# Last MoE layer of a diffusion backbone: expert results added to their tokens by one-hot products on TensorE in place of scatter and gather

## What is computed

```python
def moe(h, w_router, b_router, w_e_gate, w_e_up, w_e_down):
    ...
    gates = jnp.einsum('nk,nke->ne', w_top,
                       jax.nn.one_hot(top_idx, N_EXPERTS, dtype=jnp.float32)).astype(h.dtype)
    y = jnp.zeros_like(h)
    for e in range(N_EXPERTS):
        he = jax.nn.silu(h @ w_e_gate[e]) * (h @ w_e_up[e])
        y = y + gates[:, e:e + 1] * (he @ w_e_down[e])
    return y
```

## Time and profile before

| | |
|---|---|
| three runs, us | 1532.34, 1530.07, 1532.04 (median 1532.04) |
| profiled execution, us | 1531.17 |
| its span, us | 1529.3 |
| busy share of the span | PE 91%, DVE 52%, ACT 44%, POOL 11% |
| chain that ended last | PE 83%, DMA 7%, DVE 5%, ACT 3% |
| read from HBM, written | 341.38 MB, 25.69 MB |

### The profile page before, as it was taken

One profiled execution on the slowest core, in us unless ns is written; L12 is line 12 of the kernel. 1 busy time (PEld: TensorE's weight loads), 2 busy tenths in 40 slices (PEclk: granted clock), 3 DMA queues, 4 the chain that ended last, 5 costly groups with the idle time before them and its releaser, 6 DMA issues.

```text
span 1529.3 us, 21505 instructions
## 1 busy us (share of the span) xinstructions
PE 1395.5 (91%) x8088; PEld 1049.5 (69%) x8088; DVE 800.0 (52%) x1312; ACT 670.1 (44%) x1104; POOL 166.9 (11%) x188
## 2 busy tenths in 40 slices
PE   5699999999998995899999992999998897999995
PEld 2378777886556873778888872998885695655641
DVE  1512335424774626799999974567427665111113
ACT  3532223224665315578888864563246633000001
POOL 4210110001330000041111102000000000000001
PEclk9699999999998997799999996999999898999998
DMA  8674565334882232699999984355332158999996
GB/s 294 230 276 150 193 206 192 91 94 154 261 258 82 84 124 90 202 383 390 397 377 376 368 320 172 107 147 174 107 114 69 56 166 335 415 415 415 415 415 248
DMA packets 116054, 357.96 MB, mean 234 GB/s; under 512 B 13889, under 2 KB 14210, under 8 KB 115330
## 3 DMA queue, kind: packets, MB, share of 16 engines
q1 hardware_dynamic: 91410, 272.86, 48.6%
q0 software_dynamic: 23984, 81.85, 15.1%
q10 hardware_dynamic: 576, 2.10, 0.3%
HBM read 341.38 MB, written 25.69 MB: 240 GB/s over the span
## 4 chain that ended last, share of the span: by engine, by line
PE 83%; DMA 7%; DVE 5%; ACT 3%; issue 2%; POOL 0%; SPq 0%; POOLq 0%; DVEq 0%; ACTq 0%
PE ps L578 19%; PE ps L580 18%; PE ps L579 18%; PE ps L1194 6%; PE ps L1216 3%; PE ps L844 3%; PE ps L977 2%; PE ps L1000 2%; PE ps L1177 2%; DMA w_raw<-in_w_ada 1%; DMA ring<-in_w_e_down 1%; DMA ring<-in_w_e_up 1%; PE ps L988 1%; PE ps L1134 1%; DMA ring_h<-in_w_e_down 1%
## 5 line engine op out<-in xcount | busy, mean ns | idle before, releaser
L574 DVE TENSOR_TENSOR w_lo<-w_raw,w_hi 128x1024 fp32r<-128x1024 f32 x224 | 270.1, 1223 | 309.5 <-ACT w_hi L570 307.9
L570 ACT ACTIVATE w_hi<-w_raw 128x1024 fp32r<-128x1024 f32 x224 | 235.5, 1058 | 321.4 <-PE ps L580 317.6
L578 PE MATMUL ps<-h_hi,w_hi 128*128 128x512 f32 (+1 forms) x704 | 249.3, 354 | 11.1 <-issue 5.7
L580 PE MATMUL ps<-h_hi,w_lo 128*128 128x512 f32 (+1 forms) x704 | 247.3, 351 | 0.0
L579 PE MATMUL ps<-h_lo,w_hi 128*128 128x512 f32 (+1 forms) x704 | 247.1, 351 | 0.0
L578 PEld LDWEIGHTS ps<-h_hi,w_hi 128*128 128x128 f32 x704 | 134.2, 191 | 33.7 <-issue 9.6
L580 PEld LDWEIGHTS ps<-h_hi,w_lo 128*128 128x128 f32 x704 | 134.1, 190 | 18.7
L579 PEld LDWEIGHTS ps<-h_lo,w_hi 128*128 128x128 f32 x704 | 134.3, 191 | 18.2
L574 DVE TENSOR_TENSOR w_lo_more<-w_raw,w_hi_more 128x1024 fp32r<-128x1024 f32 x96 | 114.9, 1222 | 4.5
L570 ACT ACTIVATE w_hi_more<-w_raw 128x1024 fp32r<-128x1024 f32 x96 | 101.2, 1060 | 21.7 <-PE ps L580 19.3
L549 POOL DMA_DIRECT2D w_raw<-in_w_ada x96 | 68.8, 724 | 356.7 <-PE ps L844 350.1
(11 more groups left out here) (303 smaller groups left out, 2510.7 us busy)
## 6 DMA issues: line engine op xcount, KB each, us to landing
w_raw<-in_w_ada POOLq DMA_DIRECT2D x96, 512.0 KB, 5.5
w_raw<-in_w_e_gate SPq DMA_DIRECT2D x64, 512.0 KB
w_raw<-in_w_e_up SPq DMA_DIRECT2D x64, 512.0 KB
w_raw<-in_w_e_down SPq DMA_DIRECT2D x64, 512.0 KB
w_raw<-in_w_in SPq DMA_DIRECT2D x56, 512.0 KB
ring<-in_w_e_up SPq DMA_DIRECT2D x40, 512.0 KB, 13.7
ring<-in_w_e_gate SPq DMA_DIRECT2D x38, 512.0 KB
w_raw<-in_w_gate SPq DMA_DIRECT2D x32, 512.0 KB
```

The costliest lines, as they stand in the source:

```text
L570: act.activation(whi(n), raw[:, slot(n), :, :], ACT.Copy).then_inc(hi_ready, 1)
L574: dve.tensor_tensor(wlo(n), raw[:, slot(n), :, :], whi(n).bitcast(F32), ALU.subtract).then_inc(lo_ready, 1)
L578: pe.matmul(acc, sh, mh, start=first, stop=False, skip_group_check=True)
L580: return pe.matmul(acc, sl, mh, start=False, stop=last, skip_group_check=True)
```

## The change

All sixteen experts go back to their tokens by the product. `HELD`, `store`, `gathered`, `weighed`, the scatters, the gathers, the zeroing of `yhalf` and the row numbers in `places` go. `weigh(p)` multiplies the picks of experts 2p and 2p+1 with their gates in place, once they were used; `turn_put(p)` turns them with 8 matmuls against the identity into `put_back` (two pairs deep), and `put(e)` adds expert e's four products to banks 4 to 7, which it now holds for the whole stage. So the rest has to do with banks 0 to 3: the transposed hidden goes into the second half of bank 1, down into bank 2 alone, and all fills that a copy empties (pick half a, pick half b, row steps, turn_put) go one after the other through bank 3, in the order of a list `fills`; each waits for the copy of the one before. The picks are done in two halves.

```diff
-HELD = NE - 2
-ROWSTEPS = 10
+ROWSTEPS = 9
+FIRST_RAW = 6
...
     def r_slot(n):
         k = n % RING
-        if k < 16:
-            return ring16[:, k, :, :]
-        if k < 20:
-            return ring_h[:, k - 12, :, :]
-        if k < 26:
-            return ring_g[:, k - 20 if k < 22 else k - 18, :, :]
-        return ring_h[:, k - 26, :, :]
+        if k < 6:
+            return ring_g[:, k if k < 2 else k + 2, :, :]
+        if k < 22:
+            return ring16[:, k - FIRST_RAW, :, :]
+        return ring_h[:, k - 18 if k < 26 else k - 26, :, :]
...
-        return ps[:, 5:7, :] if t == 0 else ps[:, 3:8:4, :]
+        return ps[:, 4 + 2 * t:6 + 2 * t, :]
+
+    fills = [("a", 0), ("b", 0), ("row", 0)]
+    for e_ in range(1, NE - 1):
+        if e_ % 2:
+            fills += [("put", e_ // 2), ("a", e_ // 2 + 1), ("b", e_ // 2 + 1)]
+        elif e_ <= 8:
+            fills += [("row", e_ - 1), ("row", e_)]
+    fills.append(("put", NE // 2 - 1))
...
                 for n, (kind, e, ch) in enumerate(r_stream):
-                    if n < RAW:
-                        sp.wait_ge(lo_ready, nb - RAW + n + 1)
-                    elif n == RAW:
+                    if n == 0:
+                        sp.wait_ge(m_l[i], KT)
+                    elif FIRST_RAW <= n < FIRST_RAW + RAW:
+                        sp.wait_ge(lo_ready, nb - RAW + n - FIRST_RAW + 1)
+                    elif n == FIRST_RAW + RAW:
                         sp.wait_ge(w_used, nb)
...
-        for r in range(2 * len(tiles[1])):
-            pool.dma_start(yrows[1][r * P:(r + 1) * P, :], zrow[:, :]).then_inc(pad_out, 16)
...
                 over = pool.value_load(most[0:1, 0:1], min_val=0, max_val=T)
                 for j in range(2):
-                    pool.wait_ge(e_out[i][j], 16 * (NE // 2))
-            else:
...
+                    pool.wait_ge(e_out[j], 16 * (NE // 2))
+            pool.wait_ge(rt_loc[i], 1)
             if i:
-                over = pool.value_load(most[0:1, 0:1], min_val=0, max_val=T)
+                pool.wait_ge(z_put, 2)
+            over = pool.value_load(most[0:1, 0:1], min_val=0, max_val=T)
...
+            def turn_put(p):
+
+                take_fill(pe, ("put", p))
+                pe.wait_ge(u_weighed, p + 1)
+                for t in range(2):
+                    for j in range(2):
+                        for q in range(2):
+                            m = pe.matmul(ps[HC * q:HC * (q + 1), 3, (2 * t + j) * P:(2 * t + j + 1) * P],
+                                          pick1[:, 2 + t, 2 * p + j, :], ident, start=True, stop=True, skip_group_check=True)
+                m.then_inc(u_t, 1)
...
             def put(e):
 
                 pe.wait_ge(u_y, NE + e + 1)
-                pe.wait_ge(l_c, ROWSTEPS)
+                pe.wait_ge(*copied(("put", e // 2)))
                 for t in range(2):
                     for q in range(2):
-                        m = pe.matmul(last_bank(t)[:, q, :], put_back[HC * q:HC * (q + 1), t, e - HELD, :],
-                                      ytile1[HC * q:HC * (q + 1), e % 2, :], start=e == HELD, stop=e == NE - 1,
+                        m = pe.matmul(last_bank(t)[:, q, :], put_back[HC * q:HC * (q + 1), (e // 2) % 2, t, e % 2, :],
+                                      ytile1[HC * q:HC * (q + 1), e % 2, :], start=e == 0, stop=e == NE - 1,
                                       skip_group_check=True)
...
+            def weigh(p):
+
+                chosen = pick1[:, 2:4, 2 * p:2 * p + 2, :]
+                dve.tensor_tensor(chosen, chosen, spread(gate_of[:, :, 2 * p:2 * p + 2].unsqueeze(3), [P, 2, 2, HC]),
+                                  ALU.mult).then_inc(u_weighed, 1)
```

More of the change, by code:

```diff
@@ L304, in build @@
     starts = small("starts", [P, NE], I32)
+    gate_of = small("gate_of", [P, 2, NE])
     tokr = small("tokr", [P, 4, 2], F32R)
@@ L354, in build @@
     h_out, y_free = sem("h_out"), sem("y_free")
-    e_out = [[sem(f"e_out_{i}_{j}") for j in range(2)] for i in range(DEPTH)]
+    e_out = [sem(f"e_out_{j}") for j in range(2)]
     picked = sem("picked")
     e_in = [sem("e_in_a"), sem("e_in_b")]
-    r_in = raw_in + [sem(f"r_in{k}") for k in range(RAW, RING)]
-    r_used, l_t, l_c = sem("r_used"), sem("l_t"), sem("l_c")
+    r_new = [sem(f"r_in{k}") for k in range(RING - RAW)]
+    r_in = r_new[:FIRST_RAW] + raw_in + r_new[FIRST_RAW:]
+    r_used, u_weighed = sem("r_used"), sem("u_weighed")
     e_xt, e_xh, e_xl, e_sig, e_he, e_ht, e_hh, e_hl, e_ya, e_yd = (
@@ L757, in _ @@
                 for j in range(2):
-                    pool.wait_ge(e_out[i][j], 16 * (NE // 2))
-            else:
[L761 to L777, removed]
+                    pool.wait_ge(e_out[j], 16 * (NE // 2))
+            pool.wait_ge(rt_loc[i], 1)
             if i:
-                over = pool.value_load(most[0:1, 0:1], min_val=0, max_val=T)
+                pool.wait_ge(z_put, 2)
+            over = pool.value_load(most[0:1, 0:1], min_val=0, max_val=T)
             with pool.If(over > CAP[i]):
                 if i == 0:
-                    pool.wait_ge(pad_out, 16 * (ROWS // P))
+                    pool.wait_ge(pad_out, 16 * (ROWS // P - T // P))
                     for t in tiles[i]:
@@ L1167, in down, with pick_tokens @@
                     m.then_inc(w_used, 1)
-            def turn_pair(p):
+            def pick_tokens(side, p):
+                take_fill(pe, (side, p))
                 pe.wait_ge(picked, 4 + p // 2 + 1)
[L1171 to L1175, removed]
+                for k in range(4):
+                    kt = k if side == "a" else 4 + k
+                    d0 = (kt // CK) * CK * P + kt % CK
                     for t in tl:
-                        m = pe.matmul(ps[:, 5 + k // 4, (k % 4) * P:(k % 4 + 1) * P], h2rows[:, t - 2, d0:d0 + CK * P - 1:CK],
+                        m = pe.matmul(ps[:, 3, k * P:(k + 1) * P], h2rows[:, t - 2, d0:d0 + CK * P - 1:CK],
                                       pick1[:, t, 2 * p:2 * p + 2, :], start=t == tl[0], stop=t == tl[-1],
@@ L1221, in last_rows @@
             def last_rows(k):
[L1222 to L1223 removed]
+                take_fill(pe, ("row", k))
                 if k == 0:
@@ L1226, in last_rows @@
                         h0 = HC * (f // 4)
-                        m = pe.matmul(ps[h0:h0 + HC, 7, (f % 4) * P:(f % 4 + 1) * P], spread(mod[1][:, 40 + f, 0:1], [P, HC]), ident,
+                        m = pe.matmul(ps[h0:h0 + HC, 3, (f % 4) * P:(f % 4 + 1) * P], spread(mod[1][:, 40 + f, 0:1], [P, HC]), ident,
                                       start=True, stop=True, skip_group_check=True)
[L1229 to L1234, removed]
                 else:
@@ L1599, in tokens_a, with row_copy, put_copy @@
             def tokens_a(p):
-                act.wait_ge(u_t, NE + p + 1)
+                wait_filled(act, ("a", p))
                 if p >= 2:
                     act.wait_ge(r_used, r_done("u", 2 * p - 3))
-                act.activation(xT1[:, p % 2, 0:4, :].rearrange("p k t -> p (k t)"), ps[:, 5, :], ACT.Copy).then_inc(u_xa, 1)
+                act.activation(xT1[:, p % 2, 0:4, :].rearrange("p k t -> p (k t)"), ps[:, 3, :], ACT.Copy).then_inc(u_xa, 1)
+            def row_copy(k):
+                if k == 0:
+                    dst = ga_half[:, :]
+                else:
+                    dst = token_major[:, (k - 1) // 2, ((k - 1) % 2) * CW:((k - 1) % 2 + 1) * CW]
+                    act.wait_ge(rt_loc[i], 1)
+                wait_filled(act, ("row", k))
+                act.activation(dst, ps[:, 3, :], ACT.Copy).then_inc(u_xa, 1)
+            def put_copy(p):
+                wait_filled(act, ("put", p))
+                act.activation(put_back[:, p % 2, :, :, :].rearrange("p t j n -> p (t j n)"), ps[:, 3, :], ACT.Copy).then_inc(u_xa, 1)
             def gated1(e):
@@ L1988, in places @@
                 link(ins)
-                link(dve.tensor_tensor(v(ta), v(ta), v(tb), ALU.add))
-                for t in range(2):
-                    dve.tensor_tensor(weighed[:, t, :, :, :], spread(pick1[:, 2 + t, HELD:, :].unsqueeze(2), [P, 2, 2, HC]),
-                                      spread(ta[:, 2 + t, HELD:].unsqueeze(2).unsqueeze(3), [P, 2, 2, HC]), ALU.mult)
+                link(dve.tensor_tensor(gate_of[:, :, :], v(ta), v(tb), ALU.add))
             dve.tensor_copy(loc[:, :, t0:], loc_f[:, :, t0:])
```

139 lines of the change are left out of this document (60 added, 79 removed).

## The result

The changed kernel takes 1555.68 us in the median (1552.76 to 1558.89, four runs), beside 1531.05 us (1529.42 to 1532.34, four runs) for the kernel before. The ratio on record is 1.0175, 95% interval 1.015 to 1.0199; the quotient of the two medians is 1.0161, in the same interval. The forecast was 1559.0, range 1551 to 1570. The profiled execution took 1556.32 with a span of 1554.5, 25.2 above the span of before; the forecast made it 27.0.

What follows compares the result with a forecast made beforehand. PE was taken to bound the stage, with 12.6 us of weight waits: 26.9 + 9.2 + 1.0 + 3.2 + 0.7 - 12.6 - 1.4 = +27.0, from 1532.04 us to 1559.0, range 1551 to 1570.

Steps and rivals of the forecast that it cites:

- The bound: Last expert stage: PE decides until 1453 us, then waits for weights; a lighter DMA load gives back at most 12.6 us.
- How the 12.6 would come back: Weight transfers: dropping scatters and gathers saves 9.2 us, six earlier chunks 7.5; of 16.7 together PE keeps 12.6.
- Puts: Expert stage on PE: 14 more puts at 1.92 us, nothing hidden, +26.9; bounds 25.1 and 29.0 (one more 0.15 entry each).
- Turning the picks: Expert stage on PE: eight turn_puts at 1.22 us, less 0.59 for the old weighed step, +9.2; bounds -2.6 and +6.1.
- Halves of the picks: Picks in two halves: 0.15 us per separate entry, seven times, +1.0; bounds 0 and 2.1, if leaving costs as much.
- the one that said a put's 1.92 has both of its ends in it: Whether leaving a tiling mode is paid makes no difference for a put, whose 1.92 us runs from gate to up.
- The start: Stage start: half b waits 0.75 us for a copy, turn_put(0) 1.7, pick 1 0.7; +3.2 in all.
- rival 1: Clock: the 0.75 us break keeps PE at 1.2 GHz through gate 0 and up 0, giving 1566 us; chance 8%.
- POOL at the end of layer 0: Load of `most` moves behind the last store's wait, ahead of the gathers layer 1 waits for: +0.7 us (0 to 0.9).
- Tail: Kernel end: the first sum can start when half of the last put is done, -1.4 us (0 to 1.4).
- 2 (a put costs more in mid-stream): Each mid-stream put and turn_put costs two entries of 0.15 to 0.3 more, 24 steps: +7, 1566 us; chance 7%.
- 3 (overlap with the neighbours): Puts and turns overlap neighbouring tiles and the saved waits win, not slower; 1523 us if they cost nothing; chance 4%.

Runs made afterwards that it cites:

- third variant: Kernel before with 14 weight chunks allowed before w_out's products end, not 8, and without its 14 scatters and 4 gathers: 1516.96 us, ratio 0.9922.
- two puts variant: Changed kernel with puts for experts 14 and 15 alone, turn_puts and their copies kept: 1533.88 us, ratio 1.0035 to the kernel before.
- variant with the old ring: Changed kernel with 8 weight chunks issued before w_out's end, as in the kernel before: 1557.66 us, ratio 1.0191 to the kernel before.
- the order alone: Changed kernel with hidden transposes back behind the next gate, and places and weigh(0) ahead of hidden_copy(0): 1552.57 us, ratio 1.0167 to the kernel before.

## Why the prediction was right, point by point

- **The bound.** Right: PE's own work is 214.2 us from gate 0 to the last put (third variant), and whatever the DMA engines save is capped by the 12.4 above it (-12.6 was predicted, all of it as waits; some 1.4 of it is the low clock behind them). The changed kernel's stage is 38.8 above this floor; the sum had 39.5.
- **How the 12.6 would come back.** Half wrong, without harm to the sum. The prediction credited the two edits with 9.2 and 7.5 us. Alone they gave 11.6 and 2.35. It had not asked whether the ring had room for the early chunks: it is full before gate 0.
- **Puts.** +26.9 predicted; 1.92 each in place, 26.7 with the pair at the end (3.63 for two).
- **Turning the picks.** +9.2 predicted, 1.11 + 7 x 0.87 - 0.59 = 6.6 measured. The term was sized from L1227, and 0.87 is at the lower bound that was taken from up (0.9). L1227's 1.22 has one record of gate 1 (0.11) in it, so it was read a little too high. Its eight matmuls fill one column half after the other, turn_put alternates between the halves; that this makes the rest of the difference is likely, but no variant changed the order alone. This is the largest error of size.
- **Halves of the picks.** +1.0 predicted; 4.16 for 3.97 seven times is 1.3.
- **Missing: the ends of the new groups.** Two steps failed: the one that said a put's 1.92 has both of its ends in it, and the one that priced the halves by their entries alone and let leaving them be free. Before, each expert had one group in the dear form (up 3.60, behind the transposes) and one in the cheap form (gate 3.45, behind a down). Now both are dear: the gate follows the transposes, the up a put or half a pick. At even experts the two puts variant shows it from the other side: a put's absence gives 2.06, not 1.92. And moving the transposes back, which makes the gate 3.45 again, wins nothing in the early pairs. 14 gates at 0.15 make 2.1, and what is left of the stage's +26.4 after 26.7 + 6.6 + 1.3 + 2.15 - 12.4 is 2.0. (The 0.15 that four row steps now pay more and four transposes less do cancel, as the prediction had it.) The sum's own upper bound for the puts, one more 0.15 each, came true in its size.
- **The start.** +3.2 predicted: 0.75, 1.7 and 0.7. Measured 2.08, 1.46 and 0.69, 4.2 in all. The excess is rival 1 in part: half b stayed at 1.2 GHz (granted clock 0.50, 3.78 us for 2.15), though gate 0 ran at the high clock (1.00). The variant with the old ring, same code here, ran half b in 2.15 and needed 7.42 from pick 0 to gate 0. So this cost comes and goes with the run.
- **POOL at the end of layer 0.** +0.7 predicted, and misread: the change leaves the old load of `most` where it was and adds a second one behind the wait. The timeline of POOL, changed kernel:

```profile
918.09 0.96 POOL L765 DMA_INDIRECT ybuf<-ytile,row_of  x1 [6.65 <-DVE ytile L2113]
923.44 1.96 POOL L815 DMA_INDIRECT y<-ybuf,loc  x1 [4.39 <-issue]
925.71 0.96 POOL L815 DMA_INDIRECT y<-ybuf,loc  x1 [0.31 <-issue]
```

and the kernel before:

```profile
919.97 0.96 POOL L742 DMA_INDIRECT ybuf<-ytile,row_of  x1 [6.68 <-DVE ytile L2094]
925.86 1.42 POOL L810 DMA_INDIRECT y<-ybuf,loc  x1 [4.93 <-issue]
927.59 0.96 POOL L810 DMA_INDIRECT y<-ybuf,loc  x1 [0.31 <-issue]
```

  The second load does stand in the chain: from the landing of the last scatter to the first gather it is 1.57 us in the changed kernel and 0.99 before. But it reaches nothing that waits: the second gather is issued 7.62 us after the last scatter in both.
- **Tail.** -1.4 predicted, -1.24 measured.
- **Rivals.** 2 (a put costs more in mid-stream) is out in its size: all single puts take 1.92, and what they and the halves add around them is 2.1 us, not 7. 3 (overlap with the neighbours) is out for the puts; the turn_puts pack better than L1227 within themselves. The Trainium skill, TensorEngine Tiling (Array Packing), Key Properties, says that a change of tiling mode drains TensorE. The traces agree that a change has a price, paid on leaving a full-width group too, and put it at 0.15 us for float32 groups here, seen on gates (3.45 or 3.60), turn_puts (0.87 or 1.02), transposes (0.22 or 0.37) and downs (3.43 or 3.58).

The errors, -2.6 for the turns, +2.1 for the ends, +1.0 at the start, -0.7 on POOL, largely cancel in the total, and the late pair (31.2 forecast, 31.04 measured) hides the first two in the same way; that it came within 3.3 us of the median owes something to this luck. The medians of the kernel before, 1532.0 when I predicted and 1531.1 or 1528 beside the later runs, move by as much.

## What to carry to other kernels

Work moved from a DMA queue to an engine that is in order and already full costs its whole time there, while the freed queue gives back no more than the waits it caused; read both from the stretch where each ends last, before the edit. A head start for a ring of buffers is worth what the ring still has room for when the consumer starts, so look whether the queue would have to stop and wait for the first use. And count an engine's changes of mode, not only its instructions, when the order of small groups is moved.

## What was not expected of the hardware

- Eight float32 matmuls (64 weight columns, 128 moving) take 0.87 us where they alternate between the column halves (turn_put), and 1.22, one foreign record of 0.11 included, where four go to one half and then four to the other (L1227). They differ in their operands too, and the order was not tried alone.
- 14 scatters and 4 gathers of 3.84 MB, in 2 and 4 KB rows, cost PE 11.6 us, where their bytes at 418 GB/s are 9.2. The transfers as a whole end 9.5 us later by their bytes; the rest is an uneven end of the 16 engines and 1.4 us of low clock.
- Waits of 0.4 to 1.3 us around the last chunks are followed by a granted clock of 0.50, in the kernel before and in its variants that still wait for chunks. The two without scatters, with waits of some 0.5 there, keep 1.00 through the last down.
- The break of 0.65 us between the halves of pick 0 was followed by a half of 3.75 to 3.78 us, at the low clock, in three profiles (the changed kernel, the two puts, the order alone) and by one of 2.15 us, at the high one, in a fourth (the old ring), all of the same code. With two puts, pick 1 too ran low (0.56) behind waits of 1.46 and 0.69; in the changed kernel the same waits cost no clock (2.15 us). When the clock rises or falls is not set by the break alone.
